# Feed-forward and output projection of a hybrid decoder step: three passes of a column group in a row instead of three groups of a pass

## The reference

```python
def conv_ffn(xn, conv_prev, p):
    gate = xn @ p['ffn_w_gate']                  # 1024 -> 2752
    up = xn @ p['ffn_w_up']                      # 1024 -> 2752
    ext = jnp.concatenate([conv_prev, gate], axis=1)
    c = p['ffn_conv_b'] + sum(cw[j] * ext[:, j:j + t] for j in range(CONV_WIDTH))
    h = jax.nn.silu(c) * up
    return h @ p['ffn_w_down'], ext[:, t:]       # 2752 -> 1024
...
    x = x + jnp.concatenate([o_nsa, o_rw], axis=-1) @ p['w_out']   # 1024 -> 1024
    f, conv_new = conv_ffn(rms_norm(x, p['norm_ffn']), conv_prev, p)
    x = x + f
```

## Time and profile before

| | us |
|---|---|
| median of three runs | 4181.91 |
| lowest and highest run | 4174.9, 4185.58 |
| span of the profiled execution (first to last instruction; no other time of it is given) | 4178.0 |
| PE busy (share of the span) | 3955.0 (95%) |
| VectorE busy | 2184.5 (52%) |
| POOL busy | 1788.5 (43%) |
| ScalarE busy | 1118.1 (27%) |

### The profile page before, as it was taken

One profiled execution on the slowest core, in us unless ns is written; L12 is line 12 of the kernel. 1 busy time (PEld: TensorE's weight loads), 2 busy tenths in 40 slices (PEclk: granted clock), 3 DMA queues, 4 the chain that ended last, 5 costly groups with the idle time before them and its releaser, 6 DMA issues. The chain is left out here.

```text
span 4178.0 us, 89596 instructions
## 1 busy us (share of the span) xinstructions
PE 3955.0 (95%) x37032; PEld 3611.9 (86%) x37032; DVE 2184.5 (52%) x4925; ACT 1118.1 (27%) x2470; POOL 1788.5 (43%) x2332
## 2 busy tenths in 40 slices
PE   8998999988899999999999989999889999999998
PEld 8987888865589999999899878888656899999997
DVE  6586444468754523414456864444687454144153
ACT  3153233336541000000212523333466310000011
POOL 5532222137864444434355322122378644344342
PEclk9999999999999999999999999999999999999998
DMA  3255333220022132131323453232200321311312
GB/s 131 87 162 168 102 81 83 67 94 4 15 76 94 44 103 72 46 132 39 111 89 107 143 176 94 68 81 68 93 6 13 102 74 46 121 53 50 127 41 91
DMA packets 201960, 350.42 MB, mean 84 GB/s; under 512 B 72930, under 2 KB 135650, under 8 KB 200418
## 3 DMA queue, kind: packets, MB, share of 16 engines
q1 hardware_dynamic: 201554, 344.70, 26.2%
HBM read 253.44 MB, written 95.90 MB: 84 GB/s over the span
## 5 line engine op out<-in xcount | busy, mean ns | idle before, releaser
L2630 POOL CAST wr_hi<-wr_raw 128x256 fp32r<-128x256 f32 x584 | 262.8, 450 | 904.9 <-PE ps L2665 899.2
L2632 POOL TENSOR_TENSOR wr_lo<-wr_raw,wr_hi 128x256 fp32r<-128x256 f32 x584 | 550.3, 942 | 46.8
L2665 PE MATMUL ps<-xh,wr_hi 128*128 128x384 f32 x2064 | 453.7, 328 | 0.0
L2665 PE MATMUL ps<-xl,wr_hi 128*128 128x384 f32 x2064 | 453.1, 327 | 0.0
L2665 PE MATMUL ps<-xh,wr_lo 128*128 128x384 f32 x2064 | 452.9, 327 | 0.0
L1382 POOL TENSOR_TENSOR rc_CT<-rc_AT,rc_masks 128x256 f32<-128x256 f32 x192 | 139.0, 745 | 605.0 <-DVE rc_AT L1417 451.3
L2665 PEld LDWEIGHTS ps<-xh,wr_hi 128*128 128x128 f32 x2064 | 348.9, 188 | 0.3
L2665 PEld LDWEIGHTS ps<-xh,wr_lo 128*128 128x128 f32 x2064 | 349.0, 188 | 0.0
L2665 PEld LDWEIGHTS ps<-xl,wr_hi 128*128 128x128 f32 x2064 | 348.8, 188 | 0.0
L2718 ACT ACTIVATE de_c<-de_c 128x1088 f32<-128x1088 f32 (+1 forms) x44 | 49.0, 1114 | 1098.4 <-DVE de_c L2814 1098.4
L2665 PE MATMUL ps<-de_mixh,wr_hi 128*128 128x384 f32 (+3 forms) x1440 | 321.6, 331 | 7.9 <-DVE de_mixl L2753 7.9
(11 more groups left out here) (462 smaller groups left out, 8295.3 us busy)
## 6 DMA issues: line engine op xcount, KB each, us to landing
sa_kvp<-in_cache SPq DMA_DIRECT2D x128, 256.0 KB
scr_xres<-de_x SPq DMA_DIRECT2D x56, 544.0 KB, 2.7
de_x<-scr_xres SPq DMA_DIRECT2D x56, 544.0 KB, 3.6
wr_raw<-in_w_gate SPq DMA_DIRECT2D x42, 512.0 KB, 3.5
wr_raw<-in_w_up SPq DMA_DIRECT2D x42, 512.0 KB, 3.5
rc_arbk<-scr_arbk SPq DMA_DIRECT2D x32, 512.0 KB, 4.5
wr_raw<-in_w_down SPq DMA_DIRECT2D x32, 512.0 KB, 3.7
pr_raw<-in_w_rw SPq DMA_DIRECT2D x28, 512.0 KB, 4.3
```

Source lines behind the costliest of these rows:

```text
L2630: pool.tensor_copy(hi[:, k, :], raw[:, k, :]).then_inc(w_hi, 1)
L2632: pool.tensor_tensor(lo[:, k, :], raw[:, k, :], f32(hi[:, k, :]), ALU.subtract).then_inc(w_ready, 1)
L2665: m = pe.matmul(ps[:, (bank + b) * BANK:(bank + b) * BANK + cols], w[rows, k, :], x[rows, k, o:o + cols], start=(k == 0 and i == 0), stop= ...
```

## The change

The two inner loops of the nest change places. In each slice the nine matmuls are the same, with the same operands, banks and flags for each bank; their order is another.

```diff
-                    for i, (w, x) in enumerate(((wh, high), (wh, low), (wl, high))):
-                        for b, (o, cols) in enumerate(GROUPS):
+                    for b, (o, cols) in enumerate(GROUPS):
+                        for i, (w, x) in enumerate(((wh, high), (wh, low), (wl, high))):
                             m = pe.matmul(ps[:, (bank + b) * BANK:(bank + b) * BANK + cols], w[rows, k, :], x[rows, k, o:o + cols],
                                           start=(k == 0 and i == 0), stop=(k == kt - 1 and i == 2))
```

## The result

The changed kernel takes 4186.95 us (median of 20 runs) against 4176.78 us of the kernel before (20 runs; the first three of them gave the 4181.91 of the table ahead); the ratio is 1.0020 with an interval of 1.0012 to 1.0028. So it is slower, by 8 us by the ratio and by 10 us by the medians. The forecast was 7 us faster. The profiled execution has a span of 4185.1 us, 7.1 more than before.

The account below looks back on a forecast made before the run. The prediction took PE's streaming of matmuls to bound the two dense stages. Job ends and clock added 0, and 10512 steps x -0.7 ns gave -7 us, from 4181.9 to 4175 us, range 4155 to 4203.

Parts of the forecast that it names:

- What bounds the kernel: Two dense stages, 1757.3 us or 42% of the span: each lasts as long as its matmuls stream, 165.7 ns a step.
- The ends of a job: Start and end of each job in the dense stages: same waits, weights made in time by POOL, costed at 0.
- the rule of the Trainium skill on cycling through PSUM banks: Both dense stages: fewer bank changes would be a gain, but no lost clock to give back, so 0.
- the likeliest case: Dense stages: a step between -1.4 and +0.5 ns, time 4175 us, own range 4167 to 4187; chance 0.60.
- The step itself: Line 2665's matmuls: 10512 times the change from 165.7 ns; -0.7 ns taken, so -7 us.
- bound from below: Line 2665's step: line 524's advantage of 1.5 ns carried over in full, 10512 x -1.5 = -16 us.
- excess over columns: Part of a matmul's step beyond its columns at 2.4 GHz: 14.6 ns in line 2665, 13.1 in line 524.
- The scatter of 1.0 ns between lines 562 and 2665: Bound from above: line 562, same order and widths on other tiles, has 166.7 ns, 1.0 more; +10.5 us.
- The slow rival: Dense stages: a price for each change of the stationary tile, +12 to +23 us, middle 4199 us; chance 0.20.
- mark of 315 ns: `out` and `down` jobs: the 320-column matmul before weights change from high to low takes 315 ns, its neighbours 311 and 310.
- The fast rival: Dense stages: the excess over line 524 is wholly bank or width changes; step 164.2 ns, -16 us, 4166 us; chance 0.18.
- the much faster one: Dense stages: the whole excess is the bank change; step falls to columns plus 2.5 ns, -127 us, 4055 us; chance 0.02.

Follow-up runs that it names:

- the blocks: The changed kernel with extra matmuls at the end of layer 0's dense stage, whose sums nothing reads; the step of each sequence is read, 163.8 to 166.9 ns by distance.

## Why the prediction was wrong

*What bounds the kernel* was right: the stages last as long as their matmuls, and nearly the whole difference is 10512 times the step's. *The ends of a job* at 0 was right too: the waits and the other engines' busy time moved by no more than the step explains, and PE has no new wait. No clock was lost or given back, so the rule of the Trainium skill on cycling through PSUM banks, which the prediction weighed, had nothing to say here.

The time of 4186.95 us lies within the stated range, and even just inside the likeliest case, which ended at 4187. That is owed to the width of the range; the direction was wrong, and with it the reason.

*The step itself* failed, and in its bound from below. It read line 524's smaller excess over columns (13.1 against 14.6 ns) as what a matmul saves when bank and width stay the same, and took half of it, -0.7 ns. It measured +0.67. Three things stand in its place. The excess depends on width and place: one matmul repeated has 11.9 ns at 256 columns and 15.9 at 384, and line 524 itself falls from 13.1 to 7.0 ns in one stretch, and to 11.1 in others, when only its tiles are moved. So its advantage of 1.5 ns says nothing of what one bank in a row saves. The bank showed no gain anywhere: 0 in the old operand order, a loss of 0.2 ns or none in the new. And the order of widths, which I had counted as a small gain because there are fewer changes of width, is a loss at this place of the tiles: a slice went from 1490.0 ns to 1500.0 or 1493.3 in the `gate` and `up` jobs and from 1493.3 to 1500.0 in the others.

*The scatter of 1.0 ns between lines 562 and 2665* was put down to where the tiles lie, which is what it is, but was left as scatter. It was the larger effect of the two and could have been asked: the same order at two distances, 0 and 128. Nor was line 2665 all at one distance: its 165.9 ns in the `out` jobs against 165.6 in the `gate` and `up` jobs go with `de_mixl` at 0.

*The slow rival* had the sign and not the cause. Sequences with a single stationary part show no price for changing it, and its mark of 315 ns goes away with the place of the tiles. *The fast rival* and *the much faster one* fell with the reading of line 524. No run shows the 2.5 ns beyond the columns that the last of them was summed with; the smallest excess measured is the 7.0 ns of line 524 after its tiles were moved.

Shown by runs: that the step depends on the distance of the two tiles modulo 256 bytes, in the blocks and in the program, though the distance alone doesn't fix it; that the sign of the change depends on it too (+0.67 ns before, -0.5 ns with the two 32-byte pads, -0.2 ns at the best place). Not shown: why. That the reads of the weights and of the moving tile get in each other's way in SBUF would fit, since in the old order only their distance counted. The Trainium skill, "TensorE: Matmul & The Clock Gate", section "Step-by-step: what each phase is for", says that loading the next tile's weights doesn't steal read bandwidth from the running matmul; no run here measures that bandwidth, but the pace isn't independent of where the two lie, as moving one of them by 32 bytes changes it by up to 1.7%. Open is also why the order of widths matters at 128 and hardly at 96 or 160, and what picks one of two paces for the same order on the same tiles.

## What to carry to other kernels

When PE streams without a gap and steps of the same shape differ between two places in one trace, compare the offsets of the stationary and moving tiles before the order of the loops: here a pad was worth 20 us and the loop order at most 10, with a sign that the pad decides. Don't carry an excess per matmul from one width to another; measure one repeated matmul at the width in question. And an order tried at one placement of the tiles is tried for that placement only. Read a long stretch piece by piece before a mean is explained: here 166.3 ns was 166.7 in some jobs and 165.9 in others.

## What the runs showed of the hardware that was not expected

- Float32r matmuls of 384, 384 and 320 columns with 128-column weights, each with its load, run at 163.7 to 166.9 ns per matmul depending on the order and on the distance of the tiles modulo 256 bytes; at 192 bytes they are fastest in both orders.
- In stretches without a gap a slice of nine such matmuls, or two or four slices together, takes a whole number of 6.67 ns (1473.3, 1475.0, 1486.7, 1490.0, 1493.3 and 1500.0 ns per slice); the same order on the same tiles ran at 1493.3 in some jobs and at 1500.0 in others.
- Line 524, whose stationary tile is the activations, goes from 119.8 to 113.7 ns at 256 columns in one stretch by the same moves (its tiles then lie 64 bytes apart modulo 256 instead of 0). Other stretches of the moved kernel run at 117.8 ns, so it has two paces as well.
- 352 columns take 158.4 ns, 2.9 ns less than the middle between 320 and 384 columns (161.3).
- The long stretches of the two layers agree to about 0.02 us in eleven of the twelve kernels, so a difference of 0.1 ns per step can be read from one profile, where timing needs many runs to see 0.1%. In the twelfth, the one with passes outside and the narrow group last, they are 0.8 us or 0.2 ns a step apart; so both layers have to be read.
